# Two mixture-of-experts layers: the products with the gates go in between the tiles of the up projection, and part of VectorE's work goes to GpSimd

## The chip, the core and the metric

The kernel runs on one core of a Trainium2 chip. The metric is the device time of one execution in microseconds (us), lower is better. In this text PE is TensorE, ACT is ScalarE, DVE is VectorE, POOL is GpSimd and SP is SyncE, which here only issues loads.

## What is computed

A stack of transformer layers on 256 tokens of width 1024. Two of its layers hold the part that is changed, a lookup over 128x128 = 16384 experts; each token uses 8 heads x 16 = 128 of them:

```python
top_s, top_pos = lax.top_k(cand_s, K)
expert_idx = jnp.take_along_axis(cand_i, top_pos, axis=-1)
gates = jax.nn.softmax(top_s, axis=-1).astype(x.dtype)
...
ub = jnp.take(u, eb, axis=0)
act = jax.nn.gelu(jnp.einsum('thkd,td->thk', ub, xb), approximate=False)
vb = jnp.take(v, eb, axis=0)
return jnp.einsum('thk,thkd->td', gb * act, vb)
```

The kernel computes it densely: gelu(u x) for all 16384 experts and all tokens, times a matrix of gates that is zero except at the 128 chosen experts of a token, times v.

## The kernel before

**Tiles.** All weights come through a ring of four 512 KB tiles, loaded by SP. The experts are 128 tiles of 128 experts. For exactness each tile is split in two: ACT writes its rounded part (`take_high`, `w_hi`, L330), then DVE subtracts it from the tile (`take_low`, `w_lo`, L337). Both parts have two buffers, so `take_high` of tile j can begin once PE has begun tile j-1. PE (`split_tall`, L593, L596, L599) makes for a tile 8 products of `w_hi` with `x_hi`, 8 of `w_hi` with `x_lo`, and last 8 of `w_lo` with `x_hi`; only these wait for the subtraction. ACT turns the product into gelu (`experts`, L1135) in the big buffer `big`, one column per token. SP loads into a ring slot once the tile in it has been subtracted.

**The peer layer** (`peer`) has four stages: 1. queries and scores; 2. the 128 tiles of `u`, while DVE works out the routes (`routing`: top 16 lists, L1636 to L1645, then products of 128x2048 on L1400 and sums on L1694); with `between()` DVE puts the subtractions of tiles between the routing's instructions; 3. the gates; 4. the 128 tiles of `v`, where PE uses 512 columns (L621).

**The gates.** A token's gates lie scattered in a 128x128 matrix: gate[row, column] of its chosen experts. It is made as a product of two one-hot matrices: ACT makes `place` (|iota - column|, four tokens by four instructions, L1158, then relu(1 - that), L1165), DVE makes `gated_rows` (iota == row, times gate, L1750), PE multiplies them (L766) for four tokens, a group, into one PSUM bank, and DVE multiplies the bank into `big` (`apply_gates`, L1758). There are 64 groups to a layer; `place` and `distance` lie over `x_hi` and `x_lo`, so the stage begins when the last tile of `u` is done.

PSUM has four banks (`bank(s)`) that `SLOT_ORDER` gives out in the order of use; a user waits until the one four places before is free.

Of the kernel before, what the change touches and what calls it, by code (L numbers as in the profile page):

```python
# [65 lines left out]
LOOPED_U = EXPERT_TILES - BODY  # L66
# [57 lines left out]
def peer_slots(layer):  # L124
    return [(f"wq{layer}", 16), (f"scores{layer}", 8), (f"u{layer}", LOOPED_U), (f"routes{layer}", 2),
            (f"last_u{layer}", BODY), (f"gates{layer}", T // 4)]
# [25 lines left out]
TILE_NAMES = [name for name, n in STREAM for _ in range(n)]  # L152
SLOT = starts(SLOT_ORDER)
# [8 lines left out]
def program(nc, a, out):  # L162
    with ExitStack() as ctx:
# [16 lines left out]
        x_hi_at = nc.sbuf_base  # L180
        x_hi = sbuf("x_hi", [P, KC, T], F32R)
        x_lo_at = nc.sbuf_base
# [32 lines left out]
        gated_rows = shaped(SC[:, 0:2048], 4, 4, P)  # L215
# [3 lines left out]
        place = nc.alloc_sbuf_tensor_at("place", [P, 4, 4, P], F32, offset=x_hi_at)  # L219
        distance = nc.alloc_sbuf_tensor_at("distance", [P, 4, 4, P], F32, offset=x_lo_at)  # L220
# [21 lines left out]
        tiles_split = sem("tiles_split")  # L242
# [52 lines left out]
        distances = sem("distances")  # L295
        inner_step = sem("inner_step")
# [178 lines left out]
        def _(sp):  # L475
            def load(name, w, j):
# [3 lines left out]
                if i >= RING:  # L480
                    before = TILE_NAMES[i - RING]
                    if before in SPLIT_STAGES:
                        sp.wait_ge(tiles_split, SPLIT[before] + i - RING - TILE[before] + 1)
                    else:
                        sp.wait_ge(tiles_begun, i - RING + 2)
                sp.dma_start(tile(i)[:, 0:w.shape[2]], w[j]).then_inc(tile_landed[i % RING], 16)

            def stream(name, w):
                n, j = w.shape[0], 0
                if n >= 3 * BODY:  # L490
# [3 lines left out]
                    with sp.Fori(1, n // BODY, 1) as turns:  # L494
                        for j in range(BODY):
                            i = TILE[name] + j
                            sp.wait_ge(tiles_split, turns * BODY + (SPLIT[name] + j - RING + 1))
                            sp.dma_start(tile(i), w[ds(turns * BODY + j, 1), :, :].rearrange("a p n -> p (a n)")
                                         ).then_inc(tile_landed[i % RING], 16)
                    j = n - n % BODY  # L500
# [13 lines left out]
        def _(pool):  # L514
# [13 lines left out]
            def load_p(layer):  # L528

                moved(pool, SLOT[f"gates{layer}"], T // 4)  # L530
                pool.dma_start(pT, a[f"p{layer}"]).then_inc(p_in, 16)

            load_rows(0, (gates_split, 1))
            load_rows(1, (routes_turned, 1))
            load_p(0)
            load_rows(2)
            load_rows(3, (routes_turned, 2))
# [18 lines left out]
        def _(pe):  # L556
# [25 lines left out]
            def lo_here(name, j, turns=0):  # L582

                pe.wait_ge(tiles_split, turns * BODY + (SPLIT[name] + j + 1))
# [135 lines left out]
            def peer(layer):  # L720
# [22 lines left out]
                with pe.Fori(0, LOOPED_U // BODY, 1) as turns:  # L743
                    for j in range(BODY):
                        split_tall(f"u{layer}", j, SLOT[f"u{layer}"] + j, turns)
# [10 lines left out]
                for j in range(BODY):  # L756
                    split_tall(f"u{layer}", LOOPED_U + j, SLOT[f"last_u{layer}"] + j)

                sbase = SLOT[f"gates{layer}"]
                with pe.Fori(0, T // 16, 1) as turns:  # L760
                    for k in range(4):
                        slot_free(pe, sbase + k, turns)
                        pe.wait_ge(gate_rows, turns * 4 + (T // 4 * layer + k + 1))
                        pe.wait_ge(place_rows, turns * 4 + (T // 4 * layer + k + 1))
# [221 lines left out]
        def _(act):  # L986
# [130 lines left out]
            def peer(layer):  # L1117
# [12 lines left out]
                base = SLOT[f"u{layer}"]  # L1130

                def experts(j, turns=0):
                    s = base + j if j < LOOPED_U else SLOT[f"last_u{layer}"] + j - LOOPED_U
                    slot_here(act, s, turns * 2)
                    free(S.activation(expert_rows(j, turns), bank(s)[:, 0:T], ACT.Gelu), s)  # L1135
# [4 lines left out]
                with act.Fori(1, LOOPED_U // BODY, 1) as turns:  # L1140
# [5 lines left out]
                for j in range(LOOPED_U, EXPERT_TILES):  # L1146
                    take_high(act, f"u{layer}", j)
                    experts(j - 2)
                for j in range(EXPERT_TILES - 2, EXPERT_TILES):
                    experts(j)  # L1150
                gates = SLOT[f"gates{layer}"]

                def place_distances(k, turns):


                    slot_here(act, gates + k - 4, turns)
                    for t in range(4):
                        ins = S.activation(distance[:, k, t], iota[:], ACT.Abs,  # L1158
                                           bias=route_T[:, 1, ds(turns * 16 + (4 * k + t), 1)])
                    ins.then_inc(distances, 1)  # L1160

                def places(k, turns):

                    act.wait_ge(distances, turns * 4 + (T // 4 * layer + k + 1))
                    S.activation(place[:, k], distance[:, k], ACT.Relu, scale=-1.0, bias=1.0  # L1165
                                 ).then_inc(place_rows, 1)

# [1011 lines left out]
```

## Time and profile before

| | |
|---|---|
| three runs | 2921.97 us median (2921.3 to 2927.3) |
| profiled execution | 2922.81 us, of which 2920.0 us from the first to the last instruction |
| busy | PE 91%, DVE 60%, ACT 50%, POOL 13.8 us in all |
| granted TensorE clock | 0.967 in the mean |
| first `u` product to first `v` product | 230.34 to 717.66 us, and 1332.10 to 1819.45 us |

A share of busy time is a mean over stages with different limits, so the places of the change are read by stage: the two stretches in the last row hold stages 2 and 3.

### The profile page before, as it was taken

The numbers are of one execution on the slowest core, as the hardware profiler recorded it, in microseconds if no ns is written. First come the engines' busy times: TensorE is split into PE (matmuls) and PEld (weight loads), VectorE is DVE, ScalarE is ACT, GpSimd is POOL, SyncE is SP. The second block draws the span as 40 slices with busy tenths as digits, with TensorE's granted clock in tenths as the row PEclk, the third lists the DMA queues.
The fourth block names the chain that finished last, engine by engine and source line by source line (L and its number), as shares of the span: only waits on it lengthen the run. The fifth ranks groups of instructions, "written<-read, shape, count | busy, mean of one in ns | idle before, by whom it ended". The sixth has DMA issues, their size and how long they took to land.

```text
span 2920.0 us, 47842 instructions
## 1 busy us (share of the span) xinstructions
PE 2668.9 (91%) x16426; PEld 2368.9 (81%) x16430; DVE 1748.5 (60%) x3134; ACT 1448.4 (50%) x2435; POOL 13.8 (0%) x29
## 2 busy tenths in 40 slices
PE   8889999976999997789999976999998998988898
PEld 6689999965888876579999975888877986766796
DVE  3456777479555553346778479555555656454564
ACT  4334444488445544234444479554445535452543
POOL 0000000000000000000000000000000000000000
PEclk9899999999999998799999999999999998999999
DMA  5245555511555553145555520555555554533454
GB/s 201 67 149 174 184 182 172 180 65 33 193 194 193 192 175 95 34 149 178 180 184 170 184 80 15 194 192 193 193 172 171 183 189 146 157 101 130 144 181 150
DMA packets 123982, 446.85 MB, mean 153 GB/s; under 512 B 14280, under 2 KB 14920, under 8 KB 123648
## 3 DMA queue, kind: packets, MB, share of 16 engines
q1 hardware_dynamic: 119808, 434.16, 45.7%
q0 software_dynamic: 2608, 9.08, 1.1%
q10 hardware_dynamic: 1488, 2.59, 0.2%
q8 instruction: 45, 0.74, 0.1%
q14 instruction: 33, 0.27, 0.0%
HBM read 444.74 MB, written 1.05 MB: 153 GB/s over the span
## 4 chain that ended last, share of the span: by engine, by line
PE 80%; DVE 8%; ACT 7%; issue 3%; ACTq 1%; DMA 0%; DVEq 0%
PE ps L621 39%; PE ps L593 12%; PE ps L599 12%; PE ps L596 12%; ACT distance L1158 4%; DVE w_lo L337 1%; DVE SC L1400 1%; DVE X L1407 1%; PE ps L571 1%; PE ps L818 1%; DVE tops L1694 1%; DVE big L1407 1%; DVE x_lo L1454 1%; PE ps L736 1%; ACTq L1158 0%
## 5 line engine op out<-in xcount | busy, mean ns | idle before, releaser
L337 DVE TENSOR_TENSOR w_lo<-ring,w_hi 128x1024 fp32r<-128x1024 f32 (+1 forms) x808 | 986.3, 1222 | 910.4 <-ACT w_hi L330 899.6
L330 ACT CAST w_hi<-ring 128x1024 fp32r<-128x1024 f32 (+1 forms) x808 | 845.1, 1046 | 1108.9 <-PE ps L621 575.3
L593 PE MATMUL ps<-x_hi,w_hi 128*128 128x256 f32 x3136 | 774.6, 284 | 8.7 <-DVE x_lo L1459 4.5
L596 PE MATMUL ps<-x_lo,w_hi 128*128 128x256 f32 x3136 | 772.8, 284 | 0.0
L593 PEld LDWEIGHTS ps<-x_hi,w_hi 128*128 128x128 f32 x3136 | 604.5, 193 | 11.4 <-issue 10.5
L596 PEld LDWEIGHTS ps<-x_lo,w_hi 128*128 128x128 f32 x3136 | 604.8, 193 | 0.0
L599 PE MATMUL ps<-x_hi,w_lo 128*128 128x256 f32 x3136 | 444.1, 284 | 4.1 <-DVE w_lo L337 4.0
L621 PE MATMUL ps<-w_hi,x_hi 128*128 128x512 f32 x1488 | 414.3, 397 | 22.5 <-DVE x_lo L1454 12.5
L599 PEld LDWEIGHTS ps<-x_hi,w_lo 128*128 128x128 f32 x3136 | 406.6, 193 | 7.7 <-DVE w_lo L337 7.7
L621 PE MATMUL ps<-w_hi,x_lo 128*128 128x512 f32 x1488 | 408.3, 393 | 0.0
L621 PE MATMUL ps<-w_lo,x_hi 128*128 128x512 f32 x1488 | 406.5, 392 | 0.4 <-DVE w_lo L337 0.4
L621 PEld LDWEIGHTS ps<-w_hi,x_hi 128*128 128x128 f32 x1488 | 281.2, 192 | 88.4 <-issue 24.2
L621 PEld LDWEIGHTS ps<-w_hi,x_lo 128*128 128x128 f32 x1488 | 283.4, 191 | 60.0
L621 PEld LDWEIGHTS ps<-w_lo,x_hi 128*128 128x128 f32 x1488 | 281.6, 190 | 60.5 <-DVE w_lo L337 1.4
L766 PE MATMUL ps<-SC,place 128*128 128x128 f32 x1024 | 139.4, 286 | 80.8 <-ACT place L1165 79.1
L766 PEld LDWEIGHTS ps<-SC,place 128*128 128x128 f32 x1024 | 124.3, 195 | 96.0 <-DVE SC L1750 86.2
L1158 ACT ACTIVATE distance<-iota,tops 128x128 f32<-128x128 f32 x512 | 159.6, 396 | 0.0
L1750 DVE TENSOR_SCALAR SC<-iota,tops 128x128 f32<-128x128 f32 x512 | 141.8, 342 | 7.6 <-ACT big L1135 7.6
L1776 DVE TENSOR_TENSOR x_lo<-big,x_hi 128x256 fp32r<-128x256 f32 x256 | 107.1, 418 | 1.4 <-ACT x_hi L1180 1.4
L1180 ACT CAST x_hi<-big 128x256 fp32r (+1 forms) x256 | 103.1, 403 | 5.1 <-DVE big L1758 5.1
L1135 ACT ACTIVATE big<-ps 128x256 f32 (+1 forms) x256 | 97.2, 380 | 7.8 <-PE ps L599 7.7
L1758 DVE TENSOR_TENSOR big<-big,ps 128x512 f32 (+1 forms) x128 | 87.7, 685 | 6.0 <-PE ps L766 5.8
(221 smaller groups left out, 1509.2 us busy)
## 6 DMA issues: line engine op xcount, KB each, us to landing
ring<-in_u SPq DMA_DIRECT2D x256, 512.0 KB, 3.3
ring<-in_v SPq DMA_DIRECT2D x256, 512.0 KB, 3.3
ring<-in_ffn_in SPq DMA_DIRECT2D x88, 512.0 KB, 3.3
ring<-in_ffn_out SPq DMA_DIRECT2D x44, 512.0 KB, 3.3
ring<-in_wq SPq DMA_DIRECT2D x32, 512.0 KB, 3.3
ring<-in_ple_gate SPq DMA_DIRECT2D x16, 512.0 KB, 3.4
SC<-in_rows POOLq DMA_DIRECT2D x11, 512.0 KB, 4.5
ring<-in_a_qk SPq DMA_DIRECT2D x8, 512.0 KB, 4.7
```

The lines of the kernel that those rows point to most:

```text
L330: nc.scalar.copy(part(w_hi, i)[:, used(name)], tile(i)[:, used(name)]).then_inc(tiles_hi, 1)
L337: nc.vector.tensor_tensor(part(w_lo, i)[:, at], tile(i)[:, at], part(w_hi, i)[:, at], ALU.subtract).then_inc(tiles_split, 1)
L593: mm = nc.tensor.matmul(bank(s)[:, 0:T], hi[:, k, :], x_hi[:, k, :], start=(k == 0), stop=False)
L596: nc.tensor.matmul(bank(s)[:, 0:T], hi[:, k, :], x_lo[:, k, :], start=False, stop=False)
L599: mm = nc.tensor.matmul(bank(s)[:, 0:T], lo[:, k, :], x_hi[:, k, :], start=False, stop=(k == KC - 1))
L621: mm = nc.tensor.matmul(acc[:, 2 * tb + f, 0:cnt], x[:, k + c, tb * P:(tb + 1) * P], part(w, i)[:, at:at + cnt], start=(first and n == 0 a ...
L766: mm = nc.tensor.matmul(bank(sbase + k)[:, t * P:(t + 1) * P], place[:, k, t], gated_rows[:, k, t], start=True, stop=True)
L1135: free(S.activation(expert_rows(j, turns), bank(s)[:, 0:T], ACT.Gelu), s)
L1158: ins = S.activation(distance[:, k, t], iota[:], ACT.Abs, bias=route_T[:, 1, ds(turns * 16 + (4 * k + t), 1)])
L1180: S.copy(x_hi[:, j % BODY, :], expert_rows(j, turns)).then_inc(staged_hi, 1)
L1750: ins = V.tensor_scalar(gated_rows[:, k % 4, t], iota[:], route_T[:, 0, ds(at, 1)], route_T[:, 2, ds(at, 1)], ALU.is_equal, ALU.mult)
L1776: V.tensor_tensor(x_lo[:, j % BODY, :], expert_rows(j, turns), x_hi[:, j % BODY, :], ALU.subtract).then_inc(staged, 1)
```

## The change

In both peer layers:

- The gates' group n (four tokens) is now multiplied on PE right behind tile 52 + n of `u`, for n = 0 to 63, so behind the tiles 52 to 115. The stage of the gates is gone.
- A group meets tiles of both kinds. For the tiles that are already gelu (0 to 52 + n) DVE multiplies the bank into `big` as before. For those still to come ACT copies the bank's gates into `big` (`keep_gates`). When such a tile's product is there, ACT writes the gelu of the tokens that have their gates into a side buffer `gelus`, and DVE multiplies it into the gates there (`gate_tile`). The rest of its tokens go into `big` as before.
- `take_low` of tiles 0 to 51 and of the odd tiles from 53 to 127 is done by POOL, the rest by DVE. `between()` is gone from the routing.
- `iota - column` is now one instruction of 128x512 on POOL for a group, its absolute value and the relu one each on ACT. `gated_rows` is made by two instructions of 128x512 on DVE in place of four of 128x128. `place`, `distance`, `gated_rows` and `gelus` lie in `SC`, two buffers each.
- Only 48 tiles of `u` are in loops, where it was 120; the others are written out. In the `v` stage `stage` and `take_high`/`take_low` change places.

```diff
-LOOPED_U = EXPERT_TILES - BODY
+GROUP = 4
+GROUPS = T // GROUP
+LOOPED_U = 48
+FIRST_GROUP = 52
+EXPS_AT = 40
...
+def low_on_pool(name, j):
+
+    return name in ("u0", "u1") and (j < FIRST_GROUP or j % 2 == 1)
...
+            def experts(layer):
...
+                for j in range(LOOPED_U, EXPERT_TILES):
+                    if low_on_pool(name, j):
+                        take_low(pool, name, j)
+                    n = j - FIRST_GROUP + 2
+                    if n == 0:
+                        pool.wait_ge(routes_turned, layer + 1)
+                    if 0 <= n < GROUPS:
+
+                        if n >= 2:
+                            pool.wait_ge(place_rows, GROUPS * layer + n - 1)
+                        slots = route_T[:, 1, GROUP * n:GROUP * n + GROUP]
+                        nc.gpsimd.tensor_tensor(distance[:, n % 2], iota[:, None, :].to_broadcast([P, GROUP, P]),
+                                                slots[:, :, None].to_broadcast([P, GROUP, P]), ALU.subtract
+                                                ).then_inc(distances, 1)
...
-                sbase = SLOT[f"gates{layer}"]
-                with pe.Fori(0, T // 16, 1) as turns:
-                    for k in range(4):
...
-                        for t in range(4):
-                            mm = nc.tensor.matmul(bank(sbase + k)[:, t * P:(t + 1) * P], place[:, k, t],
-                                                  gated_rows[:, k, t], start=True, stop=True)
-                        full(mm, sbase + k)
...
+                for j in range(LOOPED_U + 2, EXPERT_TILES):
+                    split_tall(f"u{layer}", j, u_slot(layer, j))
+                    if 0 <= j - FIRST_GROUP < GROUPS:
+                        gate_group(j - FIRST_GROUP)
...
+                    if done:
+                        k = tiles_with_gates(layer, j)
+                        if k > 2:
+                            act.wait_ge(tiles_gated, k - 2)
+                        S.activation(gelus[:, j % 2, 0:done], bank(s)[:, 0:done], ACT.Gelu).then_inc(gelu_ready, 1)
...
+                for j in range(EXPS_AT, EXPERT_TILES):
                     take_high(act, f"u{layer}", j)
                     experts(j - 2)
+                    n = j - FIRST_GROUP
+                    if 0 <= n < GROUPS:
+                        places(n)
+                    if 0 <= n - 2 < GROUPS:
+                        keep_gates(n - 2)
+                    if 0 <= n + 1 < GROUPS:
+                        distances_of(n + 1)
...
+                def rows_of(n):
...
+                    tt(gated_rows[:, n % 2], iota[:, None, :].to_broadcast([P, GROUP, P]),
+                       over(route_T[:, 0, tokens]), ALU.is_equal)
+                    wait()
+                    V.tensor_tensor(gated_rows[:, n % 2], gated_rows[:, n % 2], over(route_T[:, 2, tokens]), ALU.mult
+                                    ).then_inc(gate_rows, 1)
...
+                for j in range(FIRST_GROUP, EXPERT_TILES):
+                    n = j - FIRST_GROUP
+                    if not low_on_pool(f"u{layer}", j):
+                        take_low(dve, f"u{layer}", j)
+                    if n < GROUPS:
+                        rows_of(n)
+                    if 0 <= n - 2 < GROUPS:
+                        apply_gates(n - 2)
+                    if gated_before(j - 2):
+                        gate_tile(j - 2)
```

On PE, before, the loop of the gates' stage (L766, `place` times `gated_rows`) stands behind all tiles of `u`, and the `v` stage behind it:

```order
L766 MATMUL ps<-SC,place 128x128 x4
L763 REGISTER_ALU
L766 MATMUL ps<-SC,place 128x128 x4
L763 REGISTER_ALU
L766 MATMUL ps<-SC,place 128x128 x4
L763 REGISTER_ALU
L766 MATMUL ps<-SC,place 128x128 x4
L760 REGISTER_ALU
L760 COMPARE_AND_BRANCH
L772 MATMUL ps<-zeros 128x512 x4
```

On PE, now, at one of the tiles from 52 on (L677 is the products with `w_lo`, L844 the gates' group, L671 and L674 the next tile's products with `w_hi`):

```order
L671 MATMUL ps<-x_hi,w_hi 128x256
L674 MATMUL ps<-x_lo,w_hi 128x256
L677 MATMUL ps<-x_hi,w_lo 128x256 x8
L844 MATMUL ps<-SC 128x128 x4
L671 MATMUL ps<-x_hi,w_hi 128x256
L674 MATMUL ps<-x_lo,w_hi 128x256
```

The four products of a group have moved from a loop of their own to between two tiles.

On DVE, before, at the end of the `u` stage (L337 is `take_low` of the last tiles, L1750 `gated_rows`, L1758 `apply_gates`):

```order
L337 TENSOR_TENSOR w_lo<-ring,w_hi 128x1024 x7
L1750 TENSOR_SCALAR SC<-iota,tops 128x128 x12
L1758 TENSOR_TENSOR big<-big,ps 128x128x4
L1750 TENSOR_SCALAR SC<-iota,tops 128x128 x4
L1758 TENSOR_TENSOR big<-big,ps 128x128x4
```

On DVE, now, two tiles of that stretch, an even and an odd one (L389 `take_low`, L1496 and L1823 `gated_rows`, L1832 `apply_gates`, L1840 `gate_tile`):

```order
L389 TENSOR_TENSOR w_lo<-ring,w_hi 128x1024
L1496 TENSOR_TENSOR SC<-iota,tops 128x512
L1823 TENSOR_TENSOR SC<-SC,tops 128x512
L1832 TENSOR_TENSOR big<-big,ps 128x55x4
L1840 TENSOR_TENSOR big<-SC,big 128x8
L1496 TENSOR_TENSOR SC<-iota,tops 128x512
L1823 TENSOR_TENSOR SC<-SC,tops 128x512
L1832 TENSOR_TENSOR big<-big,ps 128x56x4
L1840 TENSOR_TENSOR big<-SC,big 128x12
```

All but L1832 of these read two operands from SBUF; L1832 reads one from PSUM.

On POOL, before, nothing but loads stands between the start and the end of the peer layers (`rows` and `p`):

```order
L526 DMA SC<-in_rows 128x1024 x4
L531 DMA SC<-in_p 128x512
L526 DMA SC<-in_rows 128x1024 x4
L531 DMA SC<-in_p 128x512
```

On POOL, now, around tile 52 (L389 `take_low`, L605 the distances of a group):

```order
L389 TENSOR_TENSOR w_lo<-ring,w_hi 128x1024 x3
L605 TENSOR_TENSOR SC<-iota,tops 128x512
L389 TENSOR_TENSOR w_lo<-ring,w_hi 128x1024
L605 TENSOR_TENSOR SC<-iota,tops 128x512 x2
L389 TENSOR_TENSOR w_lo<-ring,w_hi 128x1024
```

POOL gets one subtraction of 128x1024 for each of the tiles 0 to 51, and from there for every second tile one, with two of 128x512.

## Rows read from the trace of the kernel before

**Rows 1.** The page: span, busy time by engine, busy tenths in 40 slices.

```profile
span 2920.0 us, 47842 instructions
PE 2668.9 (91%) x16426; PEld 2368.9 (81%) x16430; DVE 1748.5 (60%) x3134; ACT 1448.4 (50%) x2435; POOL 13.8 (0%) x29
...
PE   8889999976999997789999976999998998988898
```

**Rows 2.** Chain that ended last: start us, us, what.

```profile
704.64 1.27 ACT distance L1158 x4
711.39 1.27 ACT distance L1158 x4
713.33 2.04 PE ps L766 x16
717.66 348.45 PE ps L621 x1536
```

**Rows 3.** PE in order of time: first and last `u` products, both layers.

```profile
230.34 0.36 PE L593 MATMUL ps<-x_hi,w_hi 128*128 128x256 f32 x1
...
604.13 1.12 PE L599 MATMUL ps<-x_hi,w_lo 128*128 128x256 f32 x8
...
1332.10 0.36 PE L593 MATMUL ps<-x_hi,w_hi 128*128 128x256 f32 x1
...
1819.45 1.19 PE L621 MATMUL ps<-w_hi,x_hi 128*128 128x512 f32 x4 [1.45 <-ACT w_hi L330]
```

**Rows 4.** Windows: from:to length, busy PE, PEld, DVE, ACT, POOL, PEclk, DMA share, GB/s.

```profile
174.00:222.00 48.00, 47.46 (x382) 47.49 (x383) 18.55 (x16) 19.90 (x30) 0.00 (x0) 0.96 0.52 169
484.00:576.00 92.00, 91.76 (x764) 91.76 (x765) 39.33 (x34) 42.40 (x64) 0.00 (x0) 1.00 0.58 184
605.00:716.00 111.00, 70.46 (x518) 62.46 (x517) 107.16 (x320) 108.41 (x321) 0.00 (x0) 0.98 0.00 0
```

**Rows 5.** The gates' stage in order of time, one group of four tokens and more.

```profile
705.81 1.14 ACT L1165 ACTIVATE place<-distance 128x512 f32<-128x512 f32 x2
706.14 0.69 DVE L1758 TENSOR_TENSOR big<-big,ps 128x512 f32 x1
706.54 1.86 PEld L766 LDWEIGHTS ps<-SC,place 128*128 128x128 f32 x16 [0.72 <-DVE SC L1750]
706.75 1.11 DVE L1750 TENSOR_SCALAR SC<-iota,tops 128x128 f32<-128x128 f32 x4
```

**Rows 6.** Three engines late in the `u` stage, in order of time.

```profile
591.07 1.05 ACT L330 CAST w_hi<-ring 128x1024 fp32r<-128x1024 f32 x1 [1.55 <-PE ps L593]
592.02 0.38 ACT L1135 ACTIVATE big<-ps 128x256 f32<-128x256 f32 x1
...
592.15 1.23 DVE L337 TENSOR_TENSOR w_lo<-ring,w_hi 128x1024 fp32r<-128x1024 f32 x1 [1.65 <-ACT w_hi L330]
...
593.95 1.05 ACT L330 CAST w_hi<-ring 128x1024 fp32r<-128x1024 f32 x1 [1.55 <-PE ps L593]
```

**Rows 7.** DVE while it works out the routes, in order of time.

```profile
442.44 1.23 DVE L337 TENSOR_TENSOR w_lo<-ring,w_hi 128x1024 fp32r<-128x1024 f32 x1
443.58 2.29 DVE L1400 TENSOR_TENSOR SC<-SC,iota 128x2048 f32<-128x2048 f32 x1
445.79 1.22 DVE L337 TENSOR_TENSOR w_lo<-ring,w_hi 128x1024 fp32r<-128x1024 f32 x1
```

**Rows 8.** Groups by line, 225 to 610 us: busy us, mean ns, idle before.

```profile
L1640 DVE FIND_INDEX8 tops<-tops,SC 128x8 uint32<-128x128 f32 x64 | 17.1, 285 | 0.0
L1636 DVE MAX8 tops<-SC 128x8 f32<-128x128 f32 x64 | 13.9, 279 | 5.2 <-ACT SC L1128 5.2
L1640 DVE FIND_INDEX8 SC<-SC 128x8 uint32<-128x256 f32 x32 | 13.0, 419 | 0.0
...
L1400 DVE TENSOR_TENSOR SC<-SC,iota 128x2048 f32<-128x2048 f32 x4 | 9.1, 2285 | 0.0
```

**Rows 9.** Groups by line and shape on DVE and POOL, whole span.

```profile
L1776 DVE TENSOR_TENSOR x_lo<-big,x_hi 128x256 fp32r<-128x256 f32 x256 | 107.1, 418 | 1.4 <-ACT x_hi L1180 1.4
L1400 DVE TENSOR_TENSOR big<-big 128x512 f32<-128x512 f32 x16 | 10.5, 686 | 0.2
...
L516 POOL MEMSET zeros<- 128x512 bf16 x1 | 0.5, 524 | 0.3 <-POOLq L2172 0.3
```

More of the change, by code:

```diff
@@ L152, with low_counts @@
 TILE_NAMES = [name for name, n in STREAM for _ in range(n)]
+def low_on_pool(name, j):
+    return name in ("u0", "u1") and (j < FIRST_GROUP or j % 2 == 1)
+def low_counts():
+    out, done = [], [0, 0]
+    for name, n in STREAM:
+        for j in range(n if name in SPLIT_STAGES else 0):
+            k = int(low_on_pool(name, j))
+            done[k] += 1
+            out.append((k, done[k]))
+    return out
+LOW = low_counts()
 SLOT = starts(SLOT_ORDER)
@@ L744, in peer @@
                     for j in range(BODY):
-                        split_tall(f"u{layer}", j, SLOT[f"u{layer}"] + j, turns)
+                        split_tall(f"u{layer}", j, u_slot(layer, j), turns)
+                for j in range(LOOPED_U, LOOPED_U + 2):
+                    split_tall(f"u{layer}", j, u_slot(layer, j))
                 pe.wait_ge(routes_ready, layer + 1)
@@ L1145, in peer @@
                 S.activation(FV[:], FV[:], ACT.Exp).then_inc(softmax_exps, 1)
-                for j in range(LOOPED_U, EXPERT_TILES):
+                for j in range(EXPS_AT, EXPERT_TILES):
                     take_high(act, f"u{layer}", j)
                     experts(j - 2)
+                    n = j - FIRST_GROUP
[5 more added lines that the diff above has]
+                        distances_of(n + 1)
+                take_high(act, f"v{layer}", 0)
                 for j in range(EXPERT_TILES - 2, EXPERT_TILES):
                     experts(j)
[L1151 to L1166, printed above, removed]
-                act.wait_ge(routes_turned, layer + 1)
-                with act.Fori(0, T // 16, 1) as turns:
-                    place_distances(0, turns)
-                    for k in range(4):
-                        if k + 1 < 4:
-                            place_distances(k + 1, turns)
-                        places(k, turns)
-                moved(act, gates, T // 4)
                 def stage(j, turns=0):
@@ L1712, in peer @@
                 lows(f"wq{layer}", 1, 16)
-                lows(f"u{layer}", 0, 2)
                 moved(dve, SLOT[f"scores{layer}"], 8)
-                done = [2]
-                def between(now=True):
-                    if now and done[0] < LOOPED_U - BODY:
-                        take_low(dve, f"u{layer}", done[0])
-                        done[0] += 1
-                routing(layer, between)
-                while done[0] % BODY:
-                    between()
-                with dve.Fori(done[0] // BODY, LOOPED_U // BODY, 1) as turns:
-                    for j in range(BODY):
-                        take_low(dve, f"u{layer}", j, turns)
-                take_low(dve, f"u{layer}", LOOPED_U)
+                routing(layer)
                 gates_from_exps(layer)
@@ L1740, in peer @@
                 dve.sem_inc(routes_turned, 1)
-                lows(f"u{layer}", LOOPED_U + 1, EXPERT_TILES)
-                moved(dve, SLOT[f"last_u{layer}"], BODY)
-                base = SLOT[f"gates{layer}"]
-                def gate_group(k, turns=0):
-                    for t in range(4):
-                        at = turns * 16 + (4 * k + t)
-                        ins = V.tensor_scalar(gated_rows[:, k % 4, t], iota[:], route_T[:, 0, ds(at, 1)],
-                                              route_T[:, 2, ds(at, 1)], ALU.is_equal, ALU.mult)
-                    ins.then_inc(gate_rows, 1)
@@ L1769, in peer @@
-                for k in range(T // 4 - 2, T // 4):
-                    apply_gates(k)
-                moved(dve, base, T // 4)
+                def rows_of(n):
+                    if n >= 2:
+                        slot_here(dve, group_slot(layer, n - 2))
+                    tokens = slice(GROUP * n, GROUP * n + GROUP)
+                    over = lambda v: v[:, :, None].to_broadcast([P, GROUP, P])
+                    tt(gated_rows[:, n % 2], iota[:, None, :].to_broadcast([P, GROUP, P]),
[3 more added lines that the diff above has]
+                                    ).then_inc(gate_rows, 1)
@@ new lines, in apply_gates, with gate_tile @@
+                def apply_gates(n):
+                    s = group_slot(layer, n)
+                    dve.wait_ge(gates_kept, GROUPS * layer + n + 1)
+                    tiles = slice(0, FIRST_GROUP + n + 1)
+                    h = expert_tokens[:, GROUP * n:GROUP * n + GROUP, tiles].rearrange("p t e -> p e t")
+                    free(V.tensor_tensor(h, h, bank(s).rearrange("p (t e) -> p e t", t=GROUP)[:, tiles, :], ALU.mult),
+                         s)
+                def gate_tile(j):
+                    done, k = gated_before(j), tiles_with_gates(layer, j)
+                    dve.wait_ge(gelu_ready, k)
+                    h = expert_rows(j, 0)[:, 0:done]
+                    V.tensor_tensor(h, gelus[:, j % 2, 0:done], h, ALU.mult).then_inc(tiles_gated, 1)
@@ L1773, in stage @@
+                for j in range(EXPERT_TILES - 2, EXPERT_TILES):
+                    gate_tile(j)
                 def stage(j, turns=0):
```

160 lines of the change are left out of this document (94 added, 66 removed).

## The prediction

> **What bounds the kernel now.** I read the page first: PE is busy for 91% of the span, but in slices 9 and 25 of the 40 its tenths fall, and POOL does nothing to speak of, 13.8 us [rows 1]. The chain of waits says what stands in those slices. It runs through ACT's distances on L1158 in steps of 6.75 us (704.64 to 711.39), which are four groups of the gates, so 1.69 us a group; behind the last group PE takes over for the whole `v` stage, 348.45 us for 128 tiles, 2.72 each [rows 2]. The windows confirm it: in the 111 us of the gates ACT is busy 108 and DVE 107, PE's pipe only 70, and no DMA moves; in the `u` stage (484 to 576) it is PE that is never idle, 91.8 of 92 us, with DVE at 39 and ACT at 42 [rows 4]. So PE bounds `u` and `v`, and ACT with DVE bounds the gates, while PE waits.
>
> The stretch that the change rewrites goes from the first `u` product to the first `v` product: 230.34 to 717.66, 487.3 us, and 1332.10 to 1819.45, again 487.3 us [rows 3]. Its pace is 2.88 us a tile (ACT's rounding starts at 591.07 and at 593.95) [rows 6]. 128 tiles at that pace are 368.6 us; the products with `w_lo` that stand last in the view begin at 604.13 and last 1.1 us [rows 3], which makes the stage 374.9 us, so some 6 us are lost while DVE puts 2.2 us instructions between its subtractions [rows 7]. The gates and the way into `v` are the other 112.4 us.
>
> **What is removed.** The stage of the gates, 112.4 us, and the 6 us of lost steps in `u`, for each of the two layers.
>
> **What is added on PE.** A group's four products are eight weight loads and products in the trace; 16 in a row take 1.86 us and their starts are (1.86 - 0.19)/15 = 0.111 us apart [rows 5], so 0.89 us a group and 57.0 us for 64. A tile with its group then costs PE 2.88 + 0.89 = 3.77 us. The six transposes of the routes stay, 0.7 us with their waits. The unrolled code should cost nothing: the `wq` tiles are written out today and PE is busy 47.5 of 48 us there [rows 4]. From the last product to `v` there remain a gelu (0.38), the last `gate_tile`, one rounding and one subtraction of 128x256 (0.40 and 0.42), about 1.6 us with the hops. If PE sets the pace: 368.6 + 57.0 + 0.7 + 1.6 = 427.9, against 487.3, a gain of 59.4 us a layer, 119 in all.
>
> **Do the others keep up with 3.77 us?** ACT, for a tile: rounding 1.05, gelu in two parts about 0.38 + 0.2 [rows 6], absolute value and relu of 128x512 0.62 each (two relus were 1.14 together) [rows 5], the copy of 296 down to 48 gates about 0.35 by the same slope: 3.2 us. It fits. DVE, for a pair of tiles: one subtraction 1.14 (442.44 to 443.58) [rows 7], four instructions of 128x512 for `gated_rows`, 0.69 long [rows 9] and 0.61 from start to start (706.14 to 706.75) [rows 5], so 2.44, two `apply_gates` of 212 to 464 elements, about 1.0, and two `gate_tile` of 4 to 256 tokens, 0.42 at most [rows 9], about 0.5: 5.1 of 7.54 us. It fits, by itself. What is queued behind a late `gated_rows` on DVE is `apply_gates` of two groups before, which frees the bank that PE's next group but one wants, and `gate_tile`, for which ACT's gelu two tiles on waits. The slack of each is about 2 us.
>
> Ahead of tile 52, DVE only has the routing. The 14 groups of it in the view sum to 114 us, 17.1 the dearest, without the subtractions [rows 8]; begun at 231 it ends by 346, and PE wants the routes behind tile 49, at 230.3 + 50 x 2.88 = 374. 28 us of slack, so leaving out `between()` costs nothing.
>
> **POOL, the term with no row.** No row shows a subtraction on POOL. The nearest are its only long instruction, a fill of 128x512 in 0.524 us, 1.02 ns an element and one stream of data [rows 9], and DVE's subtraction, 1.23 us [rows 6]. A subtraction has two streams in and one out. Bounds for 128x1024: 1.05 us if the streams run side by side, 3.15 us if all three go in turn. I take the two reads in turn and the write beside them, 2.1 us, and 1.05 us for a distance of 128x512. For tiles 0 to 51 the rounding ends 1.15 us behind the begin of the tile before, the subtraction then at 3.3, and PE wants it at 2.88 + 1.92 = 4.8: hidden, with 1.5 us to spare. At 3.15 us it is POOL that sets the pace, some 3.25 us a tile, 19 us a layer more. The Trainium skill (GPSIMD Engine Reference, the section on performance versus the Vector engine) gives 4497 ns for an addition of 2048 elements, so 2.25 us here would be an estimate from that page; no row here can show it.
>
> **Do DVE and POOL run side by side?** This decides, and no row shows it: POOL has never read SBUF while DVE did [rows 1]. One bound is that neither slows the other; then 59 us a layer stand. The other is that whenever both want two operands from SBUF they take turns, each holding the other up for a whole instruction. Then, in a pair of tiles from 52 on, DVE's part is 1.14 + 2.44 + 0.5 = 4.1 us (`apply_gates` has an operand in PSUM and stays out), POOL's 2.1 + 2 x 1.05 = 4.2 us, and three to four handovers at the 0.1 us between two engines seen between rounding and subtraction make 0.35: 8.65 us, 4.3 a tile in place of 3.77. 64 tiles: 34 us a layer. Ahead of tile 52, ten routing instructions of 2.2 us with two operands [rows 7, 8] meet POOL's 2.1 us: two of them and a sum take 4.4 + 4.2 = 8.6 us, in which POOL does two subtractions where PE wants three, so 2.9 us go four times, less the 1.5 us at first: 10 us. The gain is then 59.4 - 34 - 10 = 15 us a layer, 31 in all.
>
> I take turns, because each of these DVE instructions asks for two operands of the full rate, and the trace gives no second path for POOL. The Trainium skill (SBUF — State Buffer, the section on who interferes with whom) states this rule: a VectorE instruction with two SBUF inputs and a GpSimd instruction that reads SBUF exclude one another, and the later one blocks for the whole length of the other. By that rule the sum is the 31 us, without it 119 us; with that page's rule and the other page's 2.25 us the pair is about 9.0 us, and the estimate comes out within a few us of no change. Nothing in this trace confirms or denies the rule.
>
> **The sum.** The profiled execution took 2922.8 us, 2920.0 of span and 2.8 around it, 0.84 above the median of the three runs. Less that and less 31: about 2891. Turns also leave gaps that neither engine can use, since POOL waits for `place` and DVE for the rounding; I put 2 us a layer on them and say 2895 us.
>
> **The rivals.**
> - *No turns.* PE sets the pace throughout: 2922 - 119 = 2803, up to 2830 if POOL has to be waited for at first. For it: DVE, ACT and POOL each fit into 3.77 us. Against it: both engines would have to draw all their operands at once. A POOL subtraction as short as 1.05 us leads here as well, turns or not (4.1 + 2.1 = 6.2 us a pair). 24%.
> - *Slower: turns, and POOL's subtraction over 2.3 us.* The place is the pair of tiles from 52 to 115. The gain is gone when these cost (59.4 - 10)/64 = 0.77 us more each, 4.54 us, 9.08 a pair; less DVE's 4.1 and 0.35 that leaves POOL 4.6, so 2.3 us for 1024 elements. At 2.6 us the pair is 9.65, 4.8 a tile, and with 14 us ahead of tile 52 a layer loses 22 us: 2965. At 3.15 us it would pass 3000. 31%.
> - *It all evens out.* The same with 2.2 to 2.3 us: 2916 to 2928. 9%.
> - *Forecast, turns at about 2.1 us:* 2850 to 2915. 36%.
>
> That the products don't move between the tiles is no rival: the order of PE shows them there.
>
> **The numbers.** Faster by over 0.2%, which is about what this kernel's runs can tell from no change, is the forecast and the first rival: 0.60. Within 0.2%: 0.09. Slower: 0.31. The range goes from the first rival's time, 2798, into the slower one as far as POOL's 2.6 us, 2965; what is left out is POOL near the upper bound. The likeliest case by itself reaches from 2850 to 2915.
>
> **What the profile of the changed kernel would show.** The chain runs on PE with pieces of L844 between those of L677. First `u` to first `v` product: 472 us by the forecast, 428 by the first rival, 490 and more by the second. POOL has 180 subtractions and 128 distances; their mean length is the first thing to read, but a length that holds a wait for DVE is too long, so it has to be read ahead of tile 40, where DVE has few instructions with two operands. With turns DVE's `take_low` and `gated_rows` last longer than 1.23 and 0.69 us in the stretch of the gates, or start late, and PE waits there for `w_lo` or `gated_rows`; without turns their lengths are those of today. Wrong would be the prediction if PE waits for ACT instead, if the routes come after tile 49, or if the written-out tiles run slower than 2.88 us with POOL and DVE in time.

## The result: 3% slower

| | median | range |
|---|---|---|
| before | 2922.3 us | 2921.3 to 2927.3, 4 runs |
| changed | 3010.89 us | 3009.28 to 3013.97, 4 runs |
| ratio | 1.0301 | 95% interval 1.0287 to 1.0315 |

The forecast was 2895 us, with 2798 to 2965 as its range. From the page of the changed kernel: span, busy time by engine, busy tenths of three engines.

```profile
span 3012.2 us, 45795 instructions
PE 2735.2 (91%) x16430; PEld 2343.3 (78%) x16430; DVE 1833.7 (61%) x2848; ACT 1398.6 (46%) x2305; POOL 666.2 (22%) x337
PE   8889899999999987889899999999997998998898
DVE  3449789984444453247959995444445655454564
POOL 0007976650000000005976651000000000000000
```

The two holes of PE (7 and 6 in slices 9 and 10, and again in 24 and 25 [rows 1]) are gone, and no slice of the two peer layers lies more than a tenth below its neighbours. Yet the span is 92 us longer. So the loss must lie in slices that look full: a PE that waits 0.3 us in every 3.3 is still a 9. The places where stages meet, PE in order of time, show which one it is (L671 is the first product of `u`, L699 of `v`, L861 what follows `v`):

```profile
230.12 0.36 PE L671 MATMUL ps<-x_hi,w_hi 128*128 128x256 f32 x1
...
687.84 1.19 PE L699 MATMUL ps<-w_hi,x_hi 128*128 128x512 f32 x4 [1.02 <-DVE x_lo L1859]
...
1110.44 1.04 PE L861 MATMUL ps<-zeros 128*128 128x512 bf16 x4
```

From the first `u` to the first `v` product it is 457.7 us, 29.6 less than the 487.3 of before [rows 3]: this part of the change gains. But from there to the end of `v` it is 422.6 us, where it was 348.45 [rows 2]: 74.2 us more. Two layers: 2 x (74.2 - 29.6) = 89 us, and the medians differ by 88.6. The cause is in the order in which ACT and DVE split a tile of weights and stage its column of tokens. The `v` stage before, in order of time (L1180 and L1776 stage a column of tokens, L330 and L337 split the weights, L621 is PE):

```profile
721.89 0.40 ACT L1180 CAST x_hi<-big 128x256 fp32r x1
722.03 1.22 DVE L337 TENSOR_TENSOR w_lo<-ring,w_hi 128x1024 fp32r<-128x1024 f32 x1 [1.18 <-ACT w_hi L330]
723.17 0.42 DVE L1776 TENSOR_TENSOR x_lo<-big,x_hi 128x256 fp32r<-128x256 f32 x1
723.24 1.07 PE L621 MATMUL ps<-w_hi,x_hi 128*128 128x512 f32 x4
```

and in the changed kernel (L1275 and L1859 stage, L377 and L389 split, L699 is PE):

```profile
761.00 1.05 ACT L377 CAST w_hi<-ring 128x1024 fp32r<-128x1024 f32 x1 [1.95 <-PE ps L699]
761.96 0.40 ACT L1275 CAST x_hi<-big 128x256 fp32r x1
762.08 1.22 DVE L389 TENSOR_TENSOR w_lo<-ring,w_hi 128x1024 fp32r<-128x1024 f32 x1 [1.74 <-ACT w_hi L377]
763.23 0.42 DVE L1859 TENSOR_TENSOR x_lo<-big,x_hi 128x256 fp32r<-128x256 f32 x1
763.78 1.18 PE L699 MATMUL ps<-w_hi,x_hi 128*128 128x512 f32 x4 [0.31 <-DVE x_lo L1859]
...
767.08 1.19 PE L699 MATMUL ps<-w_hi,x_hi 128*128 128x512 f32 x4 [0.31 <-DVE x_lo L1859]
```

Before, the 0.42 us that end at 723.6 make the column for the tile after the one that PE begins at 723.24. Now the 0.42 us that end at 763.65 make the column for the tile that begins at 763.78. Both kernels alternate the same two instructions, but the column stands one tile later, and so a ring has closed: PE begins a tile, ACT rounds the next (1.05), DVE subtracts it (1.22), then stages its column (0.42), then PE begins it. These add up to 2.69 us, and the handovers between the engines bring one turn to 767.08 - 763.78 = 3.30 us, where PE needs 2.72.

The part that I had called the deciding one, whether DVE and POOL take turns, can be read as well. DVE and POOL for two tiles in the stretch of the gates (L1496 and L1823 `gated_rows`, L1832 `apply_gates`, L1840 `gate_tile`, L605 the distances):

```profile
501.19 1.52 DVE L1496 TENSOR_TENSOR SC<-iota,tops 128x512 f32<-128x512 f32 x1
502.75 0.69 DVE L1823 TENSOR_TENSOR SC<-SC,tops 128x512 f32<-128x512 f32 x1
503.36 0.47 DVE L1832 TENSOR_TENSOR big<-big,ps 128x312 f32<-128x312 f32 x1
503.75 0.71 DVE L1840 TENSOR_TENSOR big<-SC,big 128x100 f32<-128x100 f32 x1
...
506.84 0.48 DVE L1832 TENSOR_TENSOR big<-big,ps 128x316 f32<-128x316 f32 x1
507.23 2.05 DVE L1840 TENSOR_TENSOR big<-SC,big 128x104 f32<-128x104 f32 x1
509.21 1.53 DVE L1496 TENSOR_TENSOR SC<-iota,tops 128x512 f32<-128x512 f32 x1
...
506.39 2.77 POOL L389 TENSOR_TENSOR w_lo<-ring,w_hi 128x1024 fp32r<-128x1024 f32 x1 [2.05 <-ACT w_hi L377]
509.12 1.06 POOL L605 TENSOR_TENSOR SC<-iota,tops 128x512 f32<-128x512 f32 x1
```

`gate_tile` of 104 tokens lasts 2.05 us with POOL's subtraction beside it and ends when that ends; in e3 below it takes 0.26 for 104 tokens. The first instruction of `gated_rows` lasts 1.53 in place of 0.69. POOL is held up too: this subtraction lasts 2.77 us, against 2.40 where nothing is in its way. The pair takes 509.21 - 501.19 = 8.0 us, 4.0 a tile.

### The profile page after: what moved, and what is told of

The parts are those of the page before. It is cut to its first block, busy times and chain, and to the rows that moved or that the text cites. A ratio compares the mean times of both kernels' runs of the same rounds, so it can differ in the third digit from the quotient of the medians.

```text
span 3012.2 us, 45795 instructions
## 1 busy us (share of the span) xinstructions
PE 2735.2 (91%) x16430; PEld 2343.3 (78%) x16430; DVE 1833.7 (61%) x2848; ACT 1398.6 (46%) x2305; POOL 666.2 (22%) x337
## 3 DMA queue, kind: packets, MB, share of 16 engines
HBM read 444.74 MB, written 1.05 MB: 148 GB/s over the span
## 4 chain that ended last, share of the span: by engine, by line
PE 44%; DVE 25%; issue 16%; ACT 7%; POOL 5%; DVEq 1%; ACTq 1%; DMA 0%; POOLq 0%
PE ps L699 19%; PE ps L671 6%; PE ps L677 6%; PE ps L674 6%; POOL w_lo L389 5%; DVE big L1840 5%; DVE SC L1496 4%; DVE x_lo L1859 4%; DVE w_lo L389 3%; DVE SC L1823 3%; ACT x_hi L1275 3%; ACT w_hi L377 2%; DVE big L1832 2%; DVE X L1503 1%; PE ps L649 1%
## 5 line engine op out<-in xcount | busy, mean ns | idle before, releaser
L377 ACT CAST w_hi<-ring 128x1024 fp32r<-128x1024 f32 (+1 forms) x808 | 844.3, 1045 | 1250.6 <-PE ps L699 724.9
L389 DVE TENSOR_TENSOR w_lo<-ring,w_hi 128x1024 fp32r<-128x1024 f32 x628 | 768.0, 1223 | 835.0 <-ACT w_hi L377 825.7
L671 PE MATMUL ps<-x_hi,w_hi 128*128 128x256 f32 x3136 | 784.3, 288 | 8.7 <-DVE x_lo L1555 4.4
L674 PE MATMUL ps<-x_lo,w_hi 128*128 128x256 f32 x3136 | 772.0, 284 | 0.0
L389 POOL TENSOR_TENSOR w_lo<-ring,w_hi 128x1024 fp32r<-128x1024 f32 x180 | 491.1, 2733 | 672.6 <-ACT w_hi L377 672.6
L671 PEld LDWEIGHTS ps<-x_hi,w_hi 128*128 128x128 f32 x3136 | 603.1, 192 | 11.6 <-issue 10.4
L674 PEld LDWEIGHTS ps<-x_lo,w_hi 128*128 128x128 f32 x3136 | 604.0, 193 | 0.0
L699 PE MATMUL ps<-w_hi,x_hi 128*128 128x512 f32 x1488 | 443.8, 417 | 97.6 <-DVE x_lo L1859 77.6
L677 PE MATMUL ps<-x_hi,w_lo 128*128 128x256 f32 x3136 | 444.1, 284 | 18.2 <-POOL w_lo L389 18.2
L699 PEld LDWEIGHTS ps<-w_hi,x_hi 128*128 128x128 f32 x1488 | 261.1, 192 | 251.3 <-issue 208.8
L677 PEld LDWEIGHTS ps<-x_hi,w_lo 128*128 128x128 f32 x3136 | 406.4, 193 | 22.7 <-POOL w_lo L389 22.7
L699 PE MATMUL ps<-w_hi,x_lo 128*128 128x512 f32 x1488 | 410.3, 395 | 0.0
L699 PE MATMUL ps<-w_lo,x_hi 128*128 128x512 f32 x1488 | 406.6, 392 | 0.4 <-DVE w_lo L389 0.3
L699 PEld LDWEIGHTS ps<-w_hi,x_lo 128*128 128x128 f32 x1488 | 283.7, 192 | 63.8
L699 PEld LDWEIGHTS ps<-w_lo,x_hi 128*128 128x128 f32 x1488 | 281.4, 190 | 61.8 <-DVE w_lo L389 1.3
L1840 DVE TENSOR_TENSOR big<-SC,big 128x256 f32<-128x256 f32 (+21 forms) x150 | 196.8, 1312 | 17.0 <-ACT SC L1221 17.0
L605 POOL TENSOR_TENSOR SC<-iota,tops 128x512 f32<-128x512 f32 x128 | 163.8, 1281 | 50.1 <-ACT SC L1246 47.7
L844 PE MATMUL ps<-SC 128*128 128x128 f32 x1024 | 141.2, 281 | 19.9 <-DVE big L1832 19.0
L844 PEld LDWEIGHTS ps<-SC 128*128 128x128 f32 x1024 | 124.9, 191 | 31.8 <-DVE big L1832 30.8
L1496 DVE TENSOR_TENSOR SC<-iota,tops 128x512 f32<-128x512 f32 x128 | 141.8, 1108 | 0.0
L1859 DVE TENSOR_TENSOR x_lo<-big,x_hi 128x256 fp32r<-128x256 f32 x256 | 107.1, 418 | 0.9 <-ACT x_hi L1275 0.9
```

The costliest lines, as they stand in the source:

```text
L377: nc.scalar.copy(part(w_hi, i)[:, used(name)], tile(i)[:, used(name)]).then_inc(tiles_hi, 1)
L389: eng.tensor_tensor(part(w_lo, i)[:, at], tile(i)[:, at], part(w_hi, i)[:, at], ALU.subtract).then_inc(tiles_low[LOW[n][0]], 1)
L605: nc.gpsimd.tensor_tensor(distance[:, n % 2], iota[:, None, :].to_broadcast([P, GROUP, P]), slots[:, :, None].to_broadcast([P, GROUP, P]), ...
L671: mm = nc.tensor.matmul(bank(s)[:, 0:T], hi[:, k, :], x_hi[:, k, :], start=(k == 0), stop=False)
L674: nc.tensor.matmul(bank(s)[:, 0:T], hi[:, k, :], x_lo[:, k, :], start=False, stop=False)
L677: mm = nc.tensor.matmul(bank(s)[:, 0:T], lo[:, k, :], x_hi[:, k, :], start=False, stop=(k == KC - 1))
```

## The experiments

All ratios are to the kernel before, run again on the same chip beside each experiment.

**e1_v_order_back.** The changed kernel with its order in `v` undone (the same on DVE with `take_low`):

```diff
+                stage(0)
                 with act.Fori(0, EXPERT_TILES // BODY - 1, 1) as turns:
                     for j in range(BODY):
-                        stage(j, turns)
+                        stage(j + 1, turns)
                         take_high(act, f"v{layer}", j + 1, turns)
...
```

> The changed kernel with one part of it undone: in the v stage the token columns are staged ahead of the split of the next weight tile again (stage j+1, then take_high and take_low j+1). Theory A (my reading of the two traces: the v stage went from 348.5 to 422.7 us a layer because the subtraction of the staged columns now stands behind that of the tile, 3.30 us a tile in place of 2.72): v is back at 2.72 us a tile, two layers give back 148 us, 3011 - 148 = 2863 us, which is faster than before by 2%. Rival B (v got slower because of what the new u stage leaves behind, or of the straight-line code): v stays near 3.3 us a tile and the time stays near 3010.

Measured: 2866.79 us, ratio 0.9799 (0.9783 to 0.9815). The chain of waits has the `v` stages in one piece each again:

```profile
689.43 348.46 PE ps L699 x1536
1763.55 348.45 PE ps L699 x1536
```

Theory A holds, rival B falls. Without this order the change would have been 2% faster.

**e2_before_v_swapped.** The converse, on the kernel before (and so on DVE):

```diff
-                stage(0)
+                take_high(act, f"v{layer}", 0)
                 with act.Fori(0, EXPERT_TILES // BODY - 1, 1) as turns:
                     for j in range(BODY):
-                        take_high(act, f"v{layer}", j, turns)
-                        stage(j + 1, turns)
+                        stage(j, turns)
+                        take_high(act, f"v{layer}", j + 1, turns)
...
```

> The kernel before with that one part alone: in the v stage take_high and take_low of tile j+1 stand ahead of stage j+1. Theory A: 3.30 us a tile in v, 128 x 0.58 = 74 us a layer, 2922 + 148 = 3070 us. Rival B: no change, 2922 us.

Measured: 3077.38 us, ratio 1.0519 (1.0501 to 1.0536), so 153 us more. PE waits for the staged column here too:

```profile
901.07 1.18 PE L621 MATMUL ps<-w_hi,x_hi 128*128 128x512 f32 x4 [0.29 <-DVE x_lo L1776]
```

The `v` stage takes 424.0 us, from 721.66 to 1145.62, which is 75.5 more a layer. The order alone costs it, whatever stands ahead of `v`.

**e3_lows_on_dve.** e1 with

```diff
-    return name in ("u0", "u1") and (j < FIRST_GROUP or j % 2 == 1)
+    return name in ("u0", "u1") and j < FIRST_GROUP
```

> e1 with all subtractions from tile 52 on made by DVE; POOL keeps tiles 0 to 51 and the distances. Theory T (DVE and POOL take turns when both read SBUF with DVE wanting two operands): DVE's own work is 6.2 us for a pair of tiles and it is held up by up to two distances of 1.04 us, so about 4.0 us a tile, the same as in e1: 2855 to 2875 us. Rival N (no turns; DVE was late for its own work): DVE has 3.1 us of work a tile, more than in e1, so DVE is later and the time goes above e1, or, if POOL's late subtraction was what PE waited for, PE sets the pace at 3.77 us, 64 x 0.25 x 2 = 32 us below e1.

Measured: 2836.81 us, ratio 0.9700 (0.9684 to 0.9716), 30 us below e1. That is the number of the rival, not of theory T. The windows of e1 and e3, the same stretch in both, say how (length, busy PE, PEld, DVE, ACT, POOL, clock, DMA):

```profile
395.00:655.00 260.00, 250.09 (x2061) 244.13 (x2060) 256.57 (x285) 168.89 (x383) 165.99 (x96) 1.00 0.40 133
```

```profile
395.00:655.00 260.00, 260.00 (x2199) 259.76 (x2198) 249.11 (x331) 174.94 (x393) 76.08 (x61) 1.00 0.44 143
```

PE has no hole left, so it sets the pace. But in e3 too DVE and POOL hold each other up, here at DVE's subtraction:

```profile
504.03 2.08 DVE L389 TENSOR_TENSOR w_lo<-ring,w_hi 128x1024 fp32r<-128x1024 f32 x1
...
503.99 1.04 POOL L605 TENSOR_TENSOR SC<-iota,tops 128x512 f32<-128x512 f32 x1 [1.73 <-ACT SC L1246]
```

It lasts 2.08 in place of 1.22 us: by about as much as POOL's 1.04 us reach into it. The mechanism of T is there and its price was not: giving DVE 1.14 us of work a pair took from it the 1.8 us that `gate_tile` had waited for POOL's subtraction (2.05 in place of 0.26), and more. From this run alone T and its rival could not be told apart by the time; the next four do it by the lengths.

**e4_rows_one_operand.** e1 with

```diff
...
-                    tt(gated_rows[:, n % 2], iota[:, None, :].to_broadcast([P, GROUP, P]),
-                       over(route_T[:, 0, tokens]), ALU.is_equal)
-                    wait()
-                    V.tensor_tensor(gated_rows[:, n % 2], gated_rows[:, n % 2], over(route_T[:, 2, tokens]), ALU.mult
-                                    ).then_inc(gate_rows, 1)
+                    for t in range(GROUP):
+                        at = GROUP * n + t
+                        ins = V.tensor_scalar(gated_rows[:, n % 2, t], iota[:], route_T[:, 0, at:at + 1],
+                                              route_T[:, 2, at:at + 1], ALU.is_equal, ALU.mult)
+                    ins.then_inc(gate_rows, 1)
```

> e1 with gated_rows made as in the kernel before, by four instructions of 128x128 with one tensor operand and two scalars per partition in place of two of 128x512 with two tensor operands. DVE's own time for them is the same (4 x 0.28 = 1.1 us against 1.2). Theory T1 (turns only for DVE instructions with two tensor operands from SBUF): what DVE and POOL have to share falls from 4.1 + 4.5 = 8.6 to 1.6 + 4.5 = 6.1 us a pair, PE sets the pace at 3.77 us, 64 x 0.23 x 2 = 29 us below e1: about 2834. Theory T2 (turns for these too): as e1, 2863, or slower, since each of the four can be held up by itself. Rival N (no turns at all): as e1.

Measured: 2846.09 us, ratio 0.9735 (0.9718 to 0.9753), 21 below e1 and between the theories. The group of these instructions:

```profile
L1821 DVE TENSOR_SCALAR SC<-iota,tops 128x128 f32<-128x128 f32 x252 | 132.8, 586 | 0.0
```

A mean of 586 ns, where the same instruction in the kernel before lasts 341 ns and four in a row 1.11 us [rows 5]: with one tensor operand they are held up as well, so T1 is wrong. That the time still falls by 21 us isn't foreseen by either. From group to group e4 takes 3.91 us in the mean of a layer and e1 4.05, which over 63 steps and two layers is 17 us of it. At least a part is DVE's own work, which I had taken as the same: where nothing holds them up, the four instructions take 1.02 us up to the begin of the next one, and the two in e1 take 1.32. POOL's subtraction is also held up less (2.41 us in the mean, 2.74 in e1), but its distances more (1.43 us in the mean, 1.28 in e1). What each of these gives was not tried by itself.

**e5_fill_while_routing.** On the base of e3, with `LOOPED_U` 24:

```diff
                 for j in range(LOOPED_U, EXPERT_TILES):
                     if low_on_pool(name, j):
-                        take_low(pool, name, j)
+                        i, k = TILE[name] + j, SPLIT[name] + j
+                        pool.wait_ge(tiles_hi, k + 1)
+                        nc.gpsimd.memset(part(w_lo, i).bitcast(F32), 0.0).then_inc(tiles_low[LOW[k][0]], 1)
...
```

The true low parts of these tiles are left out.

> e3 (v order of before, all subtractions from tile 52 on made by DVE) with POOL filling w_lo with zeros for the tiles 24 to 51 in place of subtracting: it then writes SBUF and reads nothing. The subtraction of these tiles is left out, so the low parts are missing there. Only 24 tiles of u are in loops. Theory T (DVE and POOL exclude each other when both read SBUF): the routing's instructions of 128x2048 with two operands, which last 4.37 us in e1 and e3, are back at 2.28 us while POOL fills, PE loses nothing ahead of tile 50 and two layers give back 2 x 11.7 = 23 us: 2814. Rival M (whatever POOL does in SBUF holds DVE up, or DVE's instructions are long for another reason): they stay over 3 us and the time near 2830.

Measured: 2816.57 us, ratio 0.9629 (0.9613 to 0.9645), 20 below e3. The time alone would not tell the two readings apart, since a fill is also shorter than a subtraction, 0.95 us against 2.40; the lengths do. The routing's instructions of 128x2048 in the changed kernel, where POOL subtracts beside them:

```profile
311.63 4.27 DVE L1496 TENSOR_TENSOR SC<-SC,iota 128x2048 f32<-128x2048 f32 x1
315.93 4.37 DVE L1496 TENSOR_TENSOR SC<-SC,tops 128x2048 f32<-128x2048 f32 x1
320.33 2.29 DVE L1782 TENSOR_REDUCE tops<-SC 128x128 f32<-128x2048 f32 x1
...
314.20 10.68 POOL L389 TENSOR_TENSOR w_lo<-ring,w_hi 128x1024 fp32r<-128x1024 f32 x3 [0.45 <-ACT w_hi L377]
```

and in e5, where it fills:

```profile
310.50 2.29 DVE L1500 TENSOR_TENSOR SC<-SC,iota 128x2048 f32<-128x2048 f32 x1
312.83 2.29 DVE L1500 TENSOR_TENSOR SC<-SC,tops 128x2048 f32<-128x2048 f32 x1
315.16 2.29 DVE L1786 TENSOR_REDUCE tops<-SC 128x128 f32<-128x2048 f32 x1
...
311.94 0.95 POOL L599 MEMSET w_lo<- 128x1024 f32 x1 [1.93 <-ACT w_hi L378]
314.83 0.95 POOL L599 MEMSET w_lo<- 128x1024 f32 x1 [1.93 <-ACT w_hi L378]
```

The fill at 311.94 lies wholly within the product that begins at 310.50, and neither is longer for it. The three subtractions from 314.20 on take 10.68 us beside the products, in place of 7.2. In the changed kernel all 16 such products of the two layers last 4.27 to 4.40 us; in e5 all of them last 2.29. The sum with one operand (L1782, L1786) is held up in neither. Theory T holds, rival M falls.

**e7_fill_odd_tiles.** e1 with the same fill for the odd tiles from 53 on.

> e1 with POOL filling w_lo with zeros for the odd tiles from 53 on in place of subtracting; it goes on reading SBUF for the distances. The subtraction of these tiles is left out. Theory T: of POOL's 4.5 us in a pair of tiles 2.1 are left that DVE has to wait for, so DVE has 5.1 + 2.1 = 7.2 us at most in a pair and PE sets the pace at 3.77 us a tile: 64 x 0.23 x 2 = 29 us below e1, 2838. Rival M: DVE is held up by the fills as well, about 1 us each; 2850 or more.

Measured: 2828.52 us, ratio 0.9674 (0.9658 to 0.9690), so T, and 10 us better than its number. Lengths under a fill (at 507.46 POOL's next distance begins, so only the first of the two stands under the fill alone):

```profile
506.66 0.69 DVE L1501 TENSOR_TENSOR SC<-iota,tops 128x512 f32<-128x512 f32 x1
507.38 0.69 DVE L1828 TENSOR_TENSOR SC<-SC,tops 128x512 f32<-128x512 f32 x1
...
506.55 0.95 POOL L600 MEMSET w_lo<- 128x1024 f32 x1 [1.68 <-ACT w_hi L377]
```

**e6_one_operand_and_fill.** e4 with the fills of e7.

> e4 (gated_rows by four instructions with one tensor operand) with the same fills as e7; the subtraction of the odd tiles from 53 on is left out. In e4 these one-operand instructions took up to 2.56 us, so something of POOL holds them too. If they are held only by what POOL reads: as e7, PE's pace, 2838. If they are held by what POOL writes too: their mean stays above 0.45 us in the stretch of the gates and the time is above e7.

Measured: 2830.85 us, ratio 0.9677 (0.9660 to 0.9693), 2.3 us above e7, whose interval of 0.9658 to 0.9690 holds it, so the two are the same as far as this can be told. The lengths tell more than the time:

```profile
500.61 2.40 DVE L1825 TENSOR_SCALAR SC<-iota,tops 128x128 f32<-128x128 f32 x4
...
500.94 0.96 POOL L600 MEMSET w_lo<- 128x1024 f32 x1 [1.67 <-ACT w_hi L377]
501.85 1.08 POOL L609 TENSOR_TENSOR SC<-iota,tops 128x512 f32<-128x512 f32 x1
...
628.24 1.83 DVE L1825 TENSOR_SCALAR SC<-iota,tops 128x128 f32<-128x128 f32 x4
...
629.00 0.98 POOL L600 MEMSET w_lo<- 128x1024 f32 x1 [5.54 <-ACT w_hi L377]
```

The first four take 2.40 us in place of 1.11, but there a distance, which reads, stands behind the fill and holds them up as well. The four that begin at 628.24 have a fill alone beside them and take 1.83: this instruction, with one tensor operand, is held up by what POOL writes too. PE sets the pace in both kernels (it is busy for all 260 us of the window 395 to 655), so it costs nothing here.

**e8_shared_while_routing.** e3, and DVE subtracts eight of the tiles ahead of 52, right ahead of the routing's eight instructions that it was held up in:

```diff
-LOOPED_U = 48
+LOOPED_U = 24
+ROUTES_AT = 50
+ROUTING_LOWS = range(28, 44, 2)
...
-    return name in ("u0", "u1") and j < FIRST_GROUP
+    return name in ("u0", "u1") and j < FIRST_GROUP and j not in ROUTING_LOWS
...
+                        take_low(dve, f"u{layer}", ROUTING_LOWS[4 * tb + 2 * k])
                         tt(c, HL[:, k, tb, :, :, None].to_broadcast([P, H8, TOPK, TOPK]),
                            iota[:, None, None, 0:TOPK].to_broadcast([P, H8, TOPK, TOPK]), ALU.is_equal)
+                        take_low(dve, f"u{layer}", ROUTING_LOWS[4 * tb + 2 * k + 1])
```

> e3 with eight of the tiles ahead of 52 (28, 30, ..., 42) subtracted by DVE between the routing's instructions of 128x2048 with two operands, where POOL's subtraction of 2.4 us and DVE's of 2.2 us got in each other's way; only 24 tiles of u are in loops. Nothing is left out. Theory T: in two tiles, 5.76 us, the turns are then 1.14 + 2.4 + 2.2 us = 5.7 with no room for handovers; PE loses some 3 to 6 us a layer in place of 11.7, so 11 to 17 us below e3: 2820 to 2826. Rival: DVE's subtractions wait behind its own long instructions, as in the kernel before, where 6 us a layer were lost, and nothing is gained: 2837.

Measured: 2811.11 us, ratio 0.9614 (0.9598 to 0.9630), the fastest of all and with nothing left out, 9 us under the lowest time that I had expected. The windows ahead of tile 50 and over the gates, and one product of the routing with POOL's subtraction:

```profile
231.00:385.00 154.00, 152.56 (x1268) 151.95 (x1267) 122.53 (x421) 74.50 (x110) 111.30 (x44) 1.00 0.57 180
395.00:655.00 260.00, 260.00 (x2199) 259.87 (x2198) 245.50 (x328) 172.58 (x386) 71.92 (x59) 1.00 0.47 144
```

```profile
314.25 2.28 DVE L1499 TENSOR_TENSOR SC<-SC,iota 128x2048 f32<-128x2048 f32 x1
...
315.68 3.12 POOL L391 TENSOR_TENSOR w_lo<-ring,w_hi 128x1024 fp32r<-128x1024 f32 x1 [3.08 <-ACT w_hi L379]
```

The turns are still there, but now DVE's product has begun first and keeps its 2.28 us, and it is POOL's subtraction that lasts longer, 3.12 us. PE loses 1.4 us of 154, and the first `v` product comes at 662.8, 431.2 us behind the first of `u` at 231.6; my bound with PE setting the pace throughout was 427.9. With 24 more tiles written out than in e3 the stage runs no slower: the long straight code costs nothing that these runs show.

## Why the prediction was wrong, point by point

1. **The step that failed** is its second paragraph: "The stretch that the change rewrites goes from the first `u` product to the first `v` product." It goes on to the end of `v`. The exchange of `stage` and `take_high` in the `v` loops, which the text ahead of the prediction lists, got neither a term nor a rival. It costs 74.2 us a layer, 148 in all, shown both ways by e1 (`v` back to 348.46 us, the time 144 us lower) and e2 (153 us more on the kernel before). All numbers for it were at hand: the loop before made a column one tile ahead; without that the way from PE to PE is 1.05 + 1.22 + 0.42 = 2.69 us and the handovers, so over 2.72.
2. **PE as the bound of `u` and `v`, ACT and DVE of the gates**: right. It is also what hid point 1: I took "PE bounds `v`" as a property of the stage, when it was one of the order in it.
3. **Gates behind the tiles cost PE 0.89 us a group, 3.77 a tile**: right. In e3, e7 and e8 PE has no hole in 260 us of that stretch, and in e3 the first and the last of the 64 groups begin at 395.20 and 633.54, 3.78 us apart in the mean.
4. **POOL's subtraction, 2.1 us taken, bounds 1.05 and 3.15**: it lasts 2.40 us undisturbed, the distance 1.04 (1.05 taken). The profile's lengths on POOL are rough, but `gate_tile` at 507.23, which waits for one, ends 0.12 us behind it. The estimate from the Trainium skill (GPSIMD Engine Reference, on performance versus the Vector engine), 2.25, was nearer than mine and still under what the trace has.
5. **Turns, taken as the case**: right, shown by e5 and e7. The rule of the Trainium skill (SBUF — State Buffer, on who interferes with whom) says that a VectorE instruction with two SBUF inputs contends with a GpSimd instruction that reads SBUF and not with one that only writes it; the runs agree with both halves, 4.37 us beside a subtraction and 2.29 beside a fill.
6. **The price of the turns**: 4.3 us a tile forecast, 4.05 measured in the mean of the 64, so 18 us a layer and not 34; POOL was slower than taken, but part of its 4.5 us a pair runs beside `apply_gates` (506.84 to 507.32 above), for which I had left no room. Ahead of tile 52 I said 10 us a layer; 50 tiles at 2.88 are 144.0, and the transposes begin at 385.82, 155.7 us behind the first product: 11.7. From the first `u` to the first `v` product I said 472 us, and it took 457.7.
7. **The sum of these parts** was 2891 us; e1, which is the changed kernel with the term that I left out taken away, is at 2866.8, in the likeliest case's own range of 2850 to 2915 and 24 us under that sum, most of it the price in point 6. The slower outcome was foreseen by another mechanism, POOL's subtraction over 2.3 us. It is over 2.3 us, and the `u` stage with the gates still gains, so that rival's point of change was wrong too: its 0.31 for "slower" came true by luck and not by its mechanism. The low end of the range, 2798, is called the first rival's time, but that rival's own sum gives 2803.

What stays open: how the 21 us of e4 divide between DVE's shorter work and the other lengths, and where the last 3 us a layer in e8 go. Of these, 2 lie ahead of the transposes, which begin at 377.60, 146.0 us behind the first product in place of 144.0.

## What to carry to other kernels

- An exchange of two lines in a loop deserves the same question as a new stage: which instruction of the next turn does each of them now stand behind, and how long is the way from the bounding engine back to itself? Add up that ring, and compare it with the engine's own time for a turn.
- Tenths and shares of busy time don't show 0.3 to 0.6 us of waiting in every 3; the time between the first instructions of two stages does, so compare that before and after for every stage, changed or not.
- Work moved to POOL is free only if DVE's instructions beside it don't want what it uses; first list which of them have two operands in SBUF, and which are of the kinds with one operand that were held up here as well (`TENSOR_SCALAR`, `CAST`).

## What the runs showed of the hardware that I had not expected

- A `TENSOR_SCALAR` of 128x128 on DVE, one tensor operand and two scalars per partition, is held up by POOL's reads (up to 2.56 us in e4, 0.34 alone) and also by its fills (four in 1.83 us in place of 1.11, e6), while a `TENSOR_TENSOR` with two operands is held up by the reads alone (0.69 us under a fill, e7). The Trainium skill (SBUF — State Buffer, on who interferes with whom) says that a `tensor_scalar` can run in a mode that takes the shared ports for itself; this agrees. A `CAST` of 128x256 from uint32 behaves the same: 0.28 us alone, 2.50 beside a subtraction of the changed kernel, 1.05 beside a fill in e5. The searches of the routing (`MAX8`, `FIND_INDEX8`) and its sums are held up by neither.
- POOL's time doesn't go by elements alone: 128x1024 from two full operands 2.40 us, 128x512 from two that are repeated along a dimension 1.04 us, a fill of 128x1024 0.95 us.
